# Hybrid decoder step: nearly every input weight unit split in two parts, the state scan in three operations a step, and the q and k rotation moved from TensorE to VectorE

## What is computed

```python
xn = rmsnorm(x, norm_mix); proj = xn @ w_in            # 2048 x 8272, in float32
u, q, k, v, qi, ki, wi, gl = split(proj)
q, k = rope(rmsnorm(q)), rope(rmsnorm(k))              # 8 q heads and 4 k heads of 128
y_att = attend(q, k, v, top-k keys chosen by qi, ki, wi)
h_t = a * h_(t-1) + b u_t  (complex, 4096 states);  y_ssm = gelu(c h + d u); y_ssm *= sigmoid(y_ssm @ w_glu)
x = x + (sigmoid(gl0) * (y_ssm @ w_branch0) + sigmoid(gl1) * (y_att @ w_branch1)) @ w_out
x = x + (silu(gate) * up) @ w_ffn_down                  # gate, up = rmsnorm(x) @ w_ffn_up
```

## Time and profile before

| | |
|---|---|
| median of 3 runs | 3066.21 us (3065.42 to 3075.17) |
| the profiled execution | 3065.53 us, of which the span is 3063.7 us |
| TensorE busy | 3006.6 us, 98% of the span |
| VectorE busy | 1956.3 us, 64% |
| ScalarE busy | 1240.4 us, 40% |
| GpSimd busy | 253.4 us, 8% |
| moved by DMA | 546.47 MB, mean 178 GB/s |
| granted clock of TensorE | 0.998 of full |

### The profile page before, as it was taken

The page is one execution under the profiler, slowest core; times in us unless marked ns, Lnnn a source line. Parts: engine busy times, 40 slices in busy tenths (PEclk is TensorE's granted clock), DMA queues, the critical chain, the costliest instruction groups (busy, mean ns, idle before and its releaser), DMA issues. The chain is left out here.

```text
span 3063.7 us, 58940 instructions
## 1 busy us (share of the span) xinstructions
PE 3006.6 (98%) x23528; PEld 2860.5 (93%) x23528; DVE 1956.3 (64%) x3397; ACT 1240.4 (40%) x1735; POOL 253.4 (8%) x239
## 2 busy tenths in 40 slices
PE   7999999999999999999999999999999999999999
PEld 7988878999999999999989888789999999999999
DVE  7559868577656545565575697785776555456553
ACT  4443333544554333434334422335435453333432
POOL 4320000400000000000043200004000000000000
PEclk9999999999999999999999999999999999999999
DMA  6447434745555655556555573347455556555564
GB/s 249 163 153 196 144 125 137 246 168 177 198 182 181 200 170 178 179 184 206 186 188 167 156 196 127 126 147 244 167 175 199 185 178 201 170 178 182 183 208 134
DMA packets 150194, 546.47 MB, mean 178 GB/s; under 512 B 19825, under 2 KB 25073, under 8 KB 149521
## 3 DMA queue, kind: packets, MB, share of 16 engines
q1 hardware_dynamic: 137296, 507.40, 49.3%
q0 software_dynamic: 12096, 35.67, 4.6%
q10 hardware_dynamic: 640, 1.16, 0.1%
HBM read 536.95 MB, written 7.21 MB: 178 GB/s over the span
## 5 line engine op out<-in xcount | busy, mean ns | idle before, releaser
L1795 DVE TENSOR_TENSOR w_ffn_low<-ring_ffn,w_ffn_high 128x1024 fp32r<-128x1024 f32 (+1 forms) x480 | 638.7, 1331 | 456.9 <-ACT w_ffn_high L1289 456.8
L1289 ACT ACTIVATE w_ffn_high<-ring_ffn 128x1024 fp32r<-128x1024 f32 (+1 forms) x480 | 548.0, 1142 | 641.7 <-PE main L1016 641.5
L1014 PE MATMUL main<-x_ffn_high,w_ffn_high 128*128 128x264 f32 x2816 | 792.5, 281 | 0.0
L1016 PE MATMUL main<-x_ffn_high,w_ffn_low 128*128 128x264 f32 x2816 | 792.1, 281 | 0.0
L1015 PE MATMUL main<-x_ffn_low,w_ffn_high 128*128 128x264 f32 x2816 | 792.1, 281 | 0.0
L1014 PEld LDWEIGHTS main<-x_ffn_high,w_ffn_high 128*128 128x128 f32 x2816 | 527.1, 187 | 0.1
L1015 PEld LDWEIGHTS main<-x_ffn_low,w_ffn_high 128*128 128x128 f32 x2816 | 527.1, 187 | 0.1
L1016 PEld LDWEIGHTS main<-x_ffn_high,w_ffn_low 128*128 128x128 f32 x2816 | 527.1, 187 | 0.0
L1014 PE MATMUL main<-hidden_high,w_ffn_high 128*128 128x264 f32 x1408 | 396.1, 281 | 0.0
L1015 PE MATMUL main<-hidden_low,w_ffn_high 128*128 128x264 f32 x1408 | 396.1, 281 | 0.0
L1016 PE MATMUL main<-hidden_high,w_ffn_low 128*128 128x264 f32 x1408 | 396.1, 281 | 0.0
(11 more groups left out here) (378 smaller groups left out, 4804.0 us busy)
## 6 DMA issues: line engine op xcount, KB each, us to landing
ring_ffn<-in_w_up SPq DMA_DIRECT2D x352, 512.0 KB, 3.3
ring<-in_w_in SPq DMA_DIRECT2D x260, 512.0 KB
ring_ffn<-in_w_down SPq DMA_DIRECT2D x128, 704.0 KB, 4.1
ring<-in_w_br SPq DMA_DIRECT2D x64, 512.0 KB
ring<-in_w_out SPq DMA_DIRECT2D x64, 512.0 KB
w_low<-in_w_in POOLq DMA_DIRECT2D x20, 512.0 KB, 7.0
ring<-in_w_glu SPq DMA_DIRECT2D x16, 512.0 KB
out_x<-x SPq DMA_DIRECT2D x8, 528.0 KB, 5.9
```

Of the source, the lines that this page charges most:

```text
L1014: mm(out, wfh[:, slot, w], high[:, kk, :], start=kk == 0, stop=False)
L1016: m = mm(out, wfl[:, slot, w], high[:, kk, :], start=False, stop=kk == chunks * kts - 1)
L1289: af(wfh[:, s, 0:cols], ring_ffn[:, s, 0:cols], ACT.Copy).then_inc(high_ready, 1)
L1795: tt(wfl[:, s, 0:cols], ring_ffn[:, s, 0:cols], wfh[:, s, 0:cols].bitcast(F32), ALU.subtract).then_inc(low_ready, 1)
```

## The change

The constants in the code say for each unit which way it is multiplied and where its high part lies. After it, 8 units of `w_in` are whole (2 to 9), 80 are split by VectorE and 42 by the adding DMA (22 of them in units 60 to 91, 20 in units 108 to 130). High parts rotate over nine places. For this the gates lie partly over `xn`, which whole units no longer read. The scan keeps tables with the coefficients doubled and signed (`step_coef`, `far_coef`), made by ScalarE in 8 copies before each scan, so that a step is one product of double length and two additions. The 12 heads are rotated by four VectorE operations each. The loads of `x` for the residual move from units 112 to 127 to units 138 to 153. Five calls of `lows_to` early in the layer ask for units sooner.

```diff
-LATE = {92: 0, 93: 1, 94: 0, 95: 1, 96: 2, 97: 3, 98: 0, 99: 2, 100: 3, 101: 0, 102: 2, 103: 3, 104: 0, 105: 2}
-BESIDE = {59: 2, 60: 0, 63: 1, 65: 2, 66: 0, 69: 1, 71: 2, 72: 0, 75: 1, 77: 2, 78: 0, 81: 1, 83: 2, 84: 0, 87: 2}
-ADDED = [60, 63, 66, 69, 72, 75, 78, 81, 84, 87]
-SPLIT = [*range(10, 56), 59, 65, 71, 77, 83, *LATE, *range(G_GLU, G_END)]
-X_AT = 112
+ADDED = [u for u in (*range(60, 92), *range(108, 131)) if (u % 3 != 2 if u < 92 else u % 6 != 5)]
+SPLIT = [u for u in (*range(10, 132), *range(G_GLU, G_END)) if u not in ADDED]
+HIGH_IN = {u: u % 4 if u < 56 or u >= 100 and u % 4 >= 2 else u % 5 if u < 100 else 5 + u % 4 for u in range(10, 118)}
+HIGH_IN |= {118: 7, 119: 3, 120: 5, 121: 6, 122: 8, 123: 3, 124: 7, 125: 5, 126: 6, 127: 8, 128: 7, 129: 5, 130: 8, 131: 7}
+X_AT = 138
...
-        gates = arena[:, 0:32 * T].rearrange("p (m t) -> p m t", t=T)
+        gates = [arena[:, (16 + m) * T:(17 + m) * T] for m in range(16)] + [xn[:, m, :] for m in range(16)]
...
+        step_coef = [a.rearrange("p (j k m) -> p j k m", j=CH, k=2) for a in (
+            vnat[:].rearrange("p b n -> p (b n)"), bbt[:, 0].rearrange("p f s -> p (f s)"))]
...
-        pw1, pw2 = tmp[:, 0:512], tmp[:, 512:1024]
+        pw = tmp[:, 0:1024]
...
+        in_high = [wih[:, at:at + KT8] for at in HIGH_AT] + [
+            whb[:, :, 0:KT8 // 2], whq[:, 0:KT8], whq[:, KT8:2 * KT8], whb[:, 1, :], wha[:]]
+
+        def parted(u):
+            return HIGH_IN.get(u) == 4
...
         def high_free(u):
 
-            if u in LATE:
-                return max((n + 1 for n in LATE if n < u and LATE[n] == LATE[u]), default=ADDED[-1] + 1)
-            if u in BESIDE:
-                return max((n + 1 for n in BESIDE if n < u and BESIDE[n] == BESIDE[u]), default=56)
-            if u < 14:
-                return 0
-            if G_GLU <= u < G_GLU + 4:
-                return G_GLU - 1 if u < G_GLU + 2 else G_GLU
+            if u in HIGH_IN:
+                first = 106 if HIGH_IN[u] == 7 else 56 if HIGH_IN[u] == 4 else 0
+                return max((n + 1 for n in HIGH_IN if n < u and HIGH_IN[n] == HIGH_IN[u]), default=first)
+            if u < G_GLU + 6:
+                return 0 if u < G_GLU + 2 else G_GLU
             return u - 3
...
-                    for t in range(12):
-                        pe.wait_ge(qnormed, t + 1)
-                        if t >= 2:
-                            pe.wait_ge(qrot_used, t - 1)
-                        mm(side[t % 2][:, 0:T], rot128, proj[:, K + t, :], start=True, stop=True).then_inc(qrot_ready, 1)
-                        if t % 3 == 1:
-                            w_in_piece(53, t // 3 * 4, 4)
+                    w_in_blocks(53, 1)
...
+                    def highs_after(done):
+
+                        while next_high < G_GLU and high_free(next_high) <= done:
+                            highs_to(next_high)
+
+                    def evac_gates(first, count, ahead=4):
                         for f in range(first, first + count):
-                            highs_to(min(2 * f + 5, ADDED[-1]))
+                            highs_to(min(2 * f + ahead, G_GLU - 1))
                             act.wait_ge(units, 2 * f + 2)
-                            af(gates[:, (f - GL + 16) % 32, :], main[f % 4][:, 0:T], ACT.Tanh, scale=0.5).then_inc(bank_free[f % 4], 1)
+                            af(gates[(f - GL + 16) % 32], main[f % 4][:, 0:T], ACT.Tanh, scale=0.5).then_inc(bank_free[f % 4], 1)
...
+                    def coefficients(half):
+
+                        tiles = slice(HALF * half, HALF * half + HALF)
+                        for near in (True, False):
+                            table = step_coef[half] if near else far_coef[:]
+                            for kind in range(2):
+                                power = apow[:, kind, :, tiles] if near else far_pow[:, :, kind, tiles]
+                                for c in range(2):
+                                    af(table[:, :, kind, c:ST:2], power, ACT.Copy, scale=-1.0 if kind and c else 1.0).then_inc(s5_copied, 1)
...
-                                evac_one(26, 0)
-                            if half == 1 and v in (9, 13, 17):
+                                evac_one(26, 2)
+                                highs_to(56)
+                            if half == 0 and v == 27:
+                                highs_to(57)
+                            if half == 1 and v in (9, 13, 17, 21, 25):
                                 highs_to(103 + v // 4 - 2)
 
+                    act.wait_ge(cneg, 1)
+                    coefficients(0)
                     act.wait_ge(pi_done, 2)
                     bu(0)
                     evac_one(27, 5)
-                    evac_proj(28, 6, 5)
+                    evac_proj(28, 6, 6)
                     act.sem_inc(proj_copied, 2)
-                    evac_gates(GL, 11)
-                    act.wait_ge(hs_saved, 1)
-                    highs_to(93)
-                    evac_gates(45, 1)
+                    evac_gates(GL, 11, 6)
+                    evac_gates(45, 1, 6)
...
+                    act.wait_ge(units, 106)
+                    coefficients(1)
+                    evac_gates(50, 4, 5)
...
+                            highs_after(2 * 54 + j + 1)
                             if j % 2 == 1:
-                                evac_gates(54 + j // 2, 1)
+                                evac_gates(54 + j // 2, 1, 0)
...
-                    lows_to(12)
+                    lows_to(13)
...
-                            lows_to(14)
+                            lows_to(15)
+                    lows_to(16)
...
-                    lows_to(16)
+                    lows_to(18)
...
-                        if n % 6 == 0 and n <= 24:
+                        if n % 3 == 0:
...
-                        spare = vnat[:] if half == 0 else bbt[:, 0].rearrange("p f s -> p (f s)").rearrange("p (b n) -> p b n", b=2)
-                        pairs = ((pw1, pw2), (spare[:, 0, :], spare[:, 1, :]))
-
-                        def products(buf, prev, coef, n):
-                            m = buf[:, 0:HALF * 2 * n].rearrange("p (s c n) -> p s c n", c=2, n=n)
-                            return m, tt(m, prev, coef.unsqueeze(2).unsqueeze(3).to_broadcast([P, HALF, 2, n]), ALU.mult)
-
-                        def fma(cur, prev, pr, pi, n):
-
-                            m1, ins = products(pw1, prev, pr, n)
-                            st.mark(ins)
-                            m2, ins = products(pw2, prev, pi, n)
-                            st.link(ins)
-                            st.link(tt(cur, cur, m1, ALU.add))
-                            st.mark(tt(cur[:, :, 0, :], cur[:, :, 0, :], m2[:, :, 1, :], ALU.subtract))
-                            st.link(tt(cur[:, :, 1, :], cur[:, :, 1, :], m2[:, :, 0, :], ALU.add))
-
-                        a1r, a1i = apow[:, 0, 0, tiles], apow[:, 1, 0, tiles]
+                        dve.wait_ge(s5_copied, 4 + 8 * (half + 1))
+
+                        def fma(cur, prev, coef, n):
+
+                            m = pw[:, 0:ST * 2 * n].rearrange("p (k m n) -> p k m n", k=2, n=n)
+                            was = prev.rearrange("p s c n -> p (s c) n").unsqueeze(1).to_broadcast([P, 2, ST, n])
+                            st.link(tt(m, was, coef.unsqueeze(3).to_broadcast([P, 2, ST, n]), ALU.mult))
+                            own, crossed = (m[:, kind].rearrange("p (s c) n -> p s c n", c=2) for kind in range(2))
+                            st.link(tt(cur, cur, own, ALU.add))
+                            st.link(tt(cur, cur, crossed[:, :, ::-1, :], ALU.add))
+
+                        near = step_coef[half]
...
                         last = hh[:, :, :, SEQ - NC:SEQ - 1]
-                        made = {}
                         for j in range(CH):
                             turn()
-                            buf1, buf2 = pairs[j % 2]
                             if j < CH - 1:
-                                m1, ins = products(buf1, last, apow[:, 0, j, tiles], NC - 1)
-                                made[j] = [m1, st.mark(ins)]
-                            if j >= 1:
-                                cur, (m, n1, w, n2) = hh[:, :, :, NC * (j - 1) + 1:NC * j], made[j - 1]
-                                st.after(n2)
-                                added = st.mark(tt(cur, cur, m, ALU.add))
-                            if j < CH - 1:
-                                if j >= 2:
-                                    st.after(done)
-                                m2, ins = products(buf2, last, apow[:, 1, j, tiles], NC - 1)
-                                made[j] += [m2, st.mark(ins)]
-                            if j >= 1:
-                                st.after(added)
-                                st.mark(tt(cur[:, :, 0, :], cur[:, :, 0, :], w[:, :, 1, :], ALU.subtract))
-                                done = st.mark(tt(cur[:, :, 1, :], cur[:, :, 1, :], w[:, :, 0, :], ALU.add))
```

(21 more changed lines are left out.)

74 lines of the change are left out of this document (37 added, 37 removed).

## The result

The changed kernel takes 3099.48 us (median of 4 runs), the kernel before, timed beside it, 3068.84 (4 runs): ratio **1.0096, interval 1.0076 to 1.0115**. It is slower by 30 us, outside the range of 3050 to 3090, and the case to which I had given 0.24. The profiled execution has a span of 3095.1 us where the one before had 3063.7, so 31.4 us are to be found.

The account below looks back on a forecast made before the run. The prediction had VectorE bound the two scans and TensorE the rest; its terms summed to +0.3 us a layer, +0.6 for two, 3066.1 against the profiled 3065.53, so 3067 us, with a range of 3050 to 3090.

Parts of the forecast that it names:

- the case to which I had given 0.24: Whole kernel: slower than the kernel before by more than 0.3%, 9.2 us; chance 0.24.
- What bounds the kernel: VectorE paces the two scans, TensorE everything elsewhere; TensorE's gain goes into waits for VectorE, some 20 us a layer.
- Term 1: Units 13 and 15: TensorE's waits of 0.79 and 1.22 us for low parts go; -2.0 us a layer.
- Term 2: Tables of the first scan: ScalarE's 8 copies before the first state input cost +1.3 us a layer (0.9 to 2.3).
- Term 3: Bisection, units 56 to 87: VectorE's added low parts and longer last-phase steps outweigh shorter turns; +7.7 us a layer.
- Term 4: Bisection's end to second state input: three steps 7.8 instead of 8.5, unit 91 shorter by 0.6; -1.3 us a layer.
- the clock: Rival: TensorE's clock falls in the 5 us gap before unit 108, total 3070 us; chance 0.05.
- Term 5: Rotation: 12 heads and 6 low parts take VectorE 26.2 us; the second scan starts 12.5 us earlier.
- Term 6: Second scan: 100.3 us of work plus 6.3 of waits, for first logits and adding DMAs; ends 2.1 us earlier.
- Term 7: Tail from second scan's end to unit 132: a 9.8 us chain follows the state output; -6.4 us against the old place.
- Term 8: DMA engines in the bisection: share rises from 0.70 to 0.95; units that come late cost +1.0 us a layer.
- The rival at 3092: Adding DMAs become the bound when crowded, in bisection and attention, some 13 us a layer; chance 0.18.

Follow-up runs that it names:

- w3: Changed kernel with units 108 to 129 left whole, without x's low part in them; ratio to the kernel before 1.0044 (1.0027 to 1.0060).
- w2: Changed kernel with units 59, 62 to 86 (ten with VectorE low parts) left whole, without x's low part; ratio to the kernel before 1.0045 (1.0030 to 1.0061).
- r3: Kernel before with only the change's early low parts (units 13, 15, 16 and 18); ratio to the kernel before 0.9983 (0.9973 to 0.9992).
- r2: Kernel before with the change's rotation of heads by VectorE and its early low parts; ratio to the kernel before 0.9922 (0.9908 to 0.9935).

## Why the prediction was wrong, by its own steps

- **What bounds the kernel: right in the main.** VectorE bounds the bisection, and w3 shows that TensorE's shorter units gain nothing in the attention. But TensorE waits for VectorE's count only 18 times in 64 units and 19.8 us in two layers, half of the 20 us a layer that I had named, and w2 shows the adding DMAs much closer behind VectorE than the sum had them.
- **Term 1, units 13 and 15 (-2.0):** measured -1.4 and -1.1. Both waits are gone; r3 gives 5 us for two layers.
- **Term 2, tables (+1.3):** TensorE waits 1.38 us behind them; the first state input starts 1.4 us earlier than before and the bisection's first sum only 0.4 (221.43 and 221.87), so +1.0.
- **Term 3, bisection (+7.7) with term 4's steps (-0.7):** 7.0 forecast from the first sum to the scan's end, 6.2 measured (346.68 and 340.92 for its last copy, less the -0.4 at the first sum). Turn and step were right to 0.02 us. The split between the two terms was not: from first to last sum it takes 113.5 us instead of 109.9, so +3.6 for the 7.7 of term 3, and the scan's end behind the last sum comes 2.6 later, where term 4 had 0.7 less. The two errors nearly cancel.
- **Term 4, TensorE behind the scan: wrong.** I had unit 91 shorter by 0.6. In truth split units 88 to 91 end early, TensorE waits 3.81 us, and unit 91 runs at the lower clock. By the row of the sums behind it (354.64 after, 346.78 before) this cost 2.1 us beyond the scan's 5.8, and 1.6 more followed ahead of the state output in layer 0, none in layer 1. The mechanism is the rival "the clock", which I had placed before unit 108, where the gap of 5 us came out as 1.92 and the clock held, not here, and priced at 3 us in all.
- **Term 5, rotation:** 26.2 forecast, 29.0 measured. I took the first two operations of a head at 0.35; all four start 0.46 apart, 12 x 0.23 = 2.8. So the scan starts 10.1 us nearer to the state input, not 12.5.
- **Term 6, second scan:** 106.6 forecast with its waits, 535.31 - 431.17 = 104.1 measured. VectorE waited 5.3 us in five places (forecast 6.3), 2.98 of it for the first logits (forecast 3.2), but nothing of note for the second ones (forecast 2.6).
- **Term 7, tail (-6.4 against the old place, -4.3 beyond the scan's): -1.1 beyond the scan's came in layer 0.** The second state output starts 1.4 us behind the scan, since unit 130 had waited 1.52 for its adding DMA, and unit 132 comes 11.7 us behind it, as before, not 9.8. VectorE makes two low parts in a row (2.35) before it, and the wait of 1.83 lowers the clock again, 1.6 us a layer.
- **Term 8, DMAs (+1.0):** about right for the bisection (1.0 us of waits in layer 0, 0.2 in layer 1), at a share of 0.91 (forecast 0.95), with the landing at 7.9 us instead of the 7.0 that I took. The least is 5.4, so the 3.2 us worked out from the Trainium skill, "DMA: Bandwidth & Descriptors", section "Anatomy of one DMA — SWDGE (gpsimd) path", are not met here either. In the attention, where term 6 had them at 3.1 in all, TensorE waited 6 us a layer for them, and without its split units (w3) that stretch is 5 us shorter.
- **What was left out, and decides: 19 us behind unit 132.** The sum went "by TensorE elsewhere", put nothing there, and took for granted that its matmuls keep their rate. The runs showed 0.1213 us a matmul in place of 0.1200, from a cause that stays open. No rival had it, though the profile before has both rates, 0.1214 in `w_in` and 0.1200 in the FFN. The rival at 3092 has nearly the right time by a mechanism that gave 13.2 us of waits at most; the number near it is a coincidence. The chance of 0.24 for "slower" was right by the same luck: 0.18 of it was that rival, most of the rest the upper edge of the forecast.

Without those 19 us the kernel would have been some 12 us slower, near 3080, inside the range, and still off the forecast of 3067, by the clock and the tail.

## What to carry to other kernels

Split a change and time its parts: here rotation and early low parts gain 24 us (r2) and the rest loses 54, 19 of them by the unexplained rate, so the sum hides both. Where another engine sets the pace, don't shorten TensorE's units: it gains nothing, it crowds the DMA engines, and a TensorE that is done too early can lose its clock for what follows; four units left whole gained some 7 us, about 4 of them by the clock. And compare the number of matmuls in a window where both kernels only run TensorE before explaining a difference by the edited stages.

## What was not expected of the hardware

- TensorE's matmuls of the same FFN loops, at a granted clock of 1.00 and with no idle time, come every 0.1200 us in ten kernels of this study and every 0.1213 in eight others, never in between, and at 0.1213 their steps repeat every five matmuls. Split units of `w_in` run at 0.1214 to 0.1215 in both kernels. Moving all tiles by 64, 512 or 768 bytes doesn't change the FFN's rate. The Trainium skill, "SBUF — State Buffer", section "Who interferes with whom", has TensorE never wait on another engine there; these runs neither show nor exclude such a cause.
- The clock fell to the lower level behind waits of 1.83, 2.07 and 3.81 us, but not behind all of them (2.03 before unit 111), and in the norms also without a wait (0.93 from 1867 to 1914 us in the kernel before). This moves the stretch from the pick to the first state output by up to 4.6 us between traces of kernels that have the same code there (before and r3, layer 0).
- The adding DMAs crowd the DMA engines early: with 22 of them in the bisection the share is 0.91, and as soon as VectorE is relieved (w2, share 0.95) TensorE's waits for them go from 13.2 to 30.3 us in both layers together.
- An operation of VectorE on 64 partitions of 264 elements takes as long as one on 128: 0.43 us.
